# The values' weight sums, loaded and stored by GpSimd's queue instead of SyncE's

## The chip, the core and the metric

The kernel runs on one core of a Trainium2 chip. The time is the device time of one execution in microseconds (us), and the figure to compare is the median over the runs. TensorE (PE) multiplies matrices; VectorE (DVE), ScalarE (ACT) and GpSimd (POOL) work on tiles in SBUF; SyncE (SP) computes nothing and issues transfers. Each engine runs its own instructions in their written order, and they meet at semaphores.

## The reference, cut to what matters

One decoder layer on 1024 positions of width 2048. A normed input `h` is multiplied by one wide matrix `w_in`; its columns are queries, keys, values and gates of two attention branches. Only the values of branch A matter here:

```python
h = rmsnorm(x, norm_w[layer])
proj = jnp.einsum('bsd,dp->bsp', h, w_in[layer])
qa, ka, va, ga, qb, kb, vb, gb = jnp.split(proj, SPLIT_IDX, axis=-1)   # va: columns 2048 to 3071
...
oa = diff_attention(qa, ka, va, lam)        # 8 heads, causal, two softmax maps each
ob = swa_sinks_attention(qb, kb, vb, sinks) # window 128, with sinks
y = jnp.concatenate([ya, yb], axis=-1)      # both gated by silu
x = x + jnp.einsum('bsm,md->bsd', y, w_out[layer])
```

## The kernel before

All products are in float32, made of three products of high and low parts: ScalarE rounds a tile to its high part (`w_hi`), VectorE subtracts it from the raw tile (`w_lo`), TensorE multiplies high by high, low by high and high by low. A part of the weights of 128 x up to 512 numbers that is loaded and split like this is a chunk.

The product `va` (1024 x 2048 by 2048 x 1024) is done with seven half-size products in place of eight, as in Strassen's and Winograd's scheme. Both operands are cut into four quarters, and some of the seven products take sums of quarters. For the weights these sums are T1 to T4 of the code (not to be mixed up with the blocks T0 to T3 below). They are made ahead, in 8 row blocks kk = 0 to 7 of 128 rows:

- `load_v_sums(kk, h)` loads 128 rows of `w_in` (h = 0: the upper half of the matrix, h = 1: the lower one), 1024 columns, 512 KB, into half h of buffer kk % 2. The buffers are `vt_buf[0]` (the trace calls it expd) and `vt_buf[1]` (w_out_sums, a name that it shares with a later use; also tbuf in the code). From kk = 2 on a load waits until the four sums of kk - 2 are stored (`vt_stored`).
- `v_weights(kk, h)` on VectorE makes two of the four sums in place, after both loads of kk have landed (`vt_in`), and counts them in `vt_done`.
- `store_v_sums(kk, h)` waits for these and stores them to DRAM (`scr_v`, in the trace w_v_sums_dram), 512 KB in rows of 2 KB.
- `load_v(j)` later fetches each sum as the weights of a tile of the product, j = 8 m + kk.

When each of these is done is written out by a table of steps. A step s is one chunk of the projection that runs on TensorE before the first attention head (`first == -1`, steps 0 to 15, then t = 16, 17 in `v_stage`). With `V_SUM_AT = [0, 2, 4, 6, 8, 11, 12, 14]` row block kk is loaded at step `V_SUM_AT[kk]`, summed two steps later and stored three steps later. In each step SyncE issues the load of a weight chunk four steps ahead (`load_ahead`), which waits until the chunk two before it is split (`w_lo_ready`); then stores and loads of the sums; then stores of gates and of rows (`store_rows`), which wait for GpSimd or ScalarE.

In the same steps the first head's queries and keys are made, in four blocks of rows, here T0 to T3. For each, VectorE reduces squares (L2164, counts `ss_ready`) and multiplies by the norm's weights, GpSimd works out the inverse root in three small instructions (`norms`: L2453, L2455, L2457), VectorE rotates the rows (`rotate`, counts `norm_chain`), and GpSimd scales them (`scale_rows`, L2490, counts `rst_ready`), after which SyncE stores them. VectorE's reduction of the next block waits for the norm of the one before it. VectorE's own order in one step is: split of a chunk, reduction, rotation, `v_weights`, sums of the left operand. Between 84 and 304 us GpSimd has nothing else to do than these norms and scalings.

Of the kernel before, what the change touches and what calls it, by code (L numbers as in the profile page):

```python
# [39 lines left out]
P = 128  # L40
# [8 lines left out]
AW = 1024  # L49
# [84 lines left out]
def v_sum_steps(*delays):  # L134

    return {t: [(kk, h) for kk in range(HALF_K) for h in range(2) if V_SUM_AT[kk] + delays[h] == t] for t in range(48)}


V_SUM_LOADS, V_SUMS, V_SUM_STORES = v_sum_steps(0, 0), v_sum_steps(2, 2), v_sum_steps(3, 3)
# [153 lines left out]
def new_kv(k, unit):  # L293

    return k == "A" or (unit - AH) % 2 == 0
# [17 lines left out]
def decoder_layer(nc, x, positions, norm_w, w_in, q_norm_a, k_norm_a, lambda_q1, lambda_k1,  # L313
# [16 lines left out]
    scr_v = nc.dram_tensor("w_v_sums_dram", (4, 1024, 512), F32).ap()  # L330

    with ExitStack() as ctx:
# [3 lines left out]
        def sem(name):  # L336
            return ctx.enter_context(nc.semaphore(name))
# [65 lines left out]
        vt_buf = [expd[:, :, :].rearrange("p a (b c) -> p (a b) c", b=2), tbuf[:, :, :]]  # L403
# [36 lines left out]
        sm = {n: sem("s_" + n) for n in names}  # L440

        def pair(name):
            return [sem(f"s_{name}{b}") for b in range(2)]
# [12 lines left out]
        vt_in, vt_stored = pair("vt_in"), pair("vt_stored")  # L456
# [65 lines left out]
        def y_time(first, s):  # L522

            return (first - (len(KINDS) - 2)) * 16 + s
# [46 lines left out]
        def _(sp):  # L571
# [16 lines left out]
                sp.dma_start(w_raw[:, s % 2, 0:nk * P].rearrange("p (k c) -> p k c", k=nk), src)\  # L588
                  .then_inc(w_in_sem[s % 2], 16)

            def load_v_sums(kk, h):

                n, r = kk % 2, kk * P
                if kk < 2:
                    sp.wait_ge(sm["w_used"], 8)
                else:
                    sp.wait_ge(vt_stored[n], 32 * (kk // 2))
                sp.dma_start(vt_buf[n][:, 2 * h:2 * h + 2, :].rearrange("p a c -> p (a c)"),
                             w_in[0, 1024 * h + r:1024 * h + r + P, 2 * AW:3 * AW]).then_inc(vt_in[n], 16)

            def store_v_sums(kk, h):
                sp.wait_ge(sm["vt_done"], 4 * kk + 2 * h + 2)
                sp.dma_start(scr_v[2 * h:2 * h + 2, kk * P:(kk + 1) * P, :].rearrange("m r t -> r m t"),
                             vt_buf[kk % 2][:, 2 * h:2 * h + 2, :]).then_inc(vt_stored[kk % 2], 16)

            def load_v(j):

                m, kk = V_TILES[j]
                x, r = V_RIGHT[m], slice(kk * P, (kk + 1) * P)
                if j < 2:  # L610
                    sp.wait_ge(sm["norm_chain"], 6)
                    sp.wait_ge(sm["ss_ready"], 2)
                else:
                    sp.wait_ge(sm["w_lo_ready"], QV + j - 3)
                if x in V_T:
                    sp.wait_ge(vt_stored[kk % 2], 32 * (kk // 2 + 1))
                    src = scr_v[V_T[x], r, :]
                else:
                    r0, c0 = V_B[x]
                    src = w_in[0, r0 + kk * P:r0 + (kk + 1) * P, 2 * AW + c0:2 * AW + c0 + 512]  # L620
                sp.dma_start(v_raw(j), src).then_inc(wide_in[(j + 2) % 4], 16)
# [8 lines left out]
            def v_stage():  # L630
                load_v(4)
                for j in range(NV):
                    for kk, h in V_SUM_STORES.get(16 + j, ()):
                        store_v_sums(kk, h)
                    for kk, h in V_SUM_LOADS.get(16 + j, ()):
                        load_v_sums(kk, h)
                    if j + 5 < NV:
                        load_v(j + 5)
                    if j >= NV - 2:
                        load_chunk(QV + j + 2, "A", 1, j - (NV - 2))  # L640
                    if j == 48:
                        load_step("A", 0, 0)
                    for r in range(4):
                        if j == 35 + r:
                            store_v(u_y, 0, 0, r, 1 + 2 * r, "v_first_stored")
                        if j == 43 + r:
                            store_v(u_y, 0, 1, r, 9 + r, "v_first_stored")
                for q in (2, 3):
                    load_chunk(QV + NV + q, "A", 1, q)
                for r in range(4):  # L650
                    store_v(u_z, 512, 1, r, 16 + 2 * r + 1, "v_stored")
                    store_v(u_x, 512, 0, r, 16 + 2 * r + 2, "v_stored")
# [286 lines left out]
            def body(it, first):  # L939
                for s in range(16):  # L940
                    i = s // 2
                    d, ch, before = proj_tile(it, first, s)
                    t = y_time(first, s)
# [3 lines left out]
                    if first == len(KINDS) - 1 and s == 0:  # L947
                        load_step(kind(first), it, 1)
                    load_ahead(it, first, s)
                    for kk, h in V_SUM_STORES.get(s, ()) if first == -1 else ():  # L950
                        store_v_sums(kk, h)
                    for kk, h in V_SUM_LOADS.get(s, ()) if first == -1 else ():
                        load_v_sums(kk, h)
                    if first == len(KINDS) and s == 1:
                        store_y(step_at(-1, it, first), it, first)
                    if d and ch["last"] and d["kind"] != "O" and not d["turned"]:
# [1477 lines left out]
        def _(pool):  # L2434
# [34 lines left out]
                x_rms(r)  # L2469

            def v_stage():
                pool.wait_ge(sm["w_used"], QV + NV)
                for c in range(2):
                    pool.memset(kT_lo[c][half_rows[1 - c], :].bitcast(F32), 0.0).then_inc(sm["k_zeros"], 1)
                    pool.wait_ge(sm["k_zeros"], c + 1)
# [6 lines left out]
            def scale_rows(d, b):  # L2482

                if not d["norm"]:
                    return
                seq = d["K"] * 2 + b
                wait(pool, sm["norm_chain"], seq * 3 + 3)
                wait(pool, sm["rs_ready"], seq * 3 + 3)
                x3 = rows[:, b, :].rearrange("p (g c) -> p g c", g=8)
                pool.tensor_tensor(x3, x3, ss_h[:, 16:24].unsqueeze(2).to_broadcast([P, 8, HD]), ALU.mult)\  # L2490
                    .then_inc(rst_ready[b], 1)

            def lo_v(st):

                i, k = st["i"], st["k"]
                if not new_kv(k, st["unit"]):
                    return
                lo, w = (2 * P, P) if k == "A" else (3 * P, HD)
                wait(pool, sm["v_hi_ready"], v_count(k, st["unit"], i))

                dst = v_lo[:, i, :] if k == "A" else v_hi[:, i, HD:P]
                pool.tensor_tensor(dst, qkv[:, i % 2, lo:lo + w], v_hi[:, i, 0:w].bitcast(F32),
                                   ALU.subtract).then_inc(sm["v_split"], 1)

            def sum_s3(k):

# [35 lines left out]
            def body(it, first):  # L2542
                for s in range(16):
                    i = s // 2
                    cur = step_at(i, it, first)
                    back1 = step_at(i - 1, it, first)
                    last = first == len(KINDS) - 1
                    if s % 2 and last or s % 2 == 0 and cur and cur["k"] == "A" and i:
                        lo_v(cur)
                    if s % 2 and cur and cur["k"] == "B":  # L2550
                        scale_probs(cur)
                    tb = turned_before(it, first, s)
                    if tb and tb[0]["norm"]:
                        norms(tb[0], tb[2])
                    if s % 2:
                        if back1 and back1["k"] == "A":
                            wait(pool, sm["o_squared"], back1["G"] + 1)
                            inv_rms(ss_o[:, 2:3], ss_o[:, 1:2], ss_o[:, 0:1], 4, sm["o_pow"], back1["G"] * 4)
                            wait(pool, sm["o_pow"], back1["G"] * 4 + 3)
                            pool.tensor_tensor(ss_o[:, 0:1], ss_o[:, 0:1], inv_sum[:, back1["i"] % 2, 0:1], ALU.mult)\  # L2560
                                .then_inc(sm["o_pow"], 1)
                        if cur and not last and not (cur["k"] == "A" and i):
                            lo_v(cur)
                    late = norm_block_back(it, first, s, 1)
                    if tb and not norm_block_back(it, first, s, 0):
                        scale_rows(tb[0], tb[2])
                    if late:
                        scale_rows(late[0], 1)
                    for k in S3_LOWS.get(s, ()) if first == len(KINDS) - 1 else ():
                        s3_low(k)  # L2570
                    for what, k, m in sum_steps(first, s):
                        if what == "S3" and m:
                            sum_s3(k)
                        elif what == "S" and 2 <= m < 5:
                            sum_s(k, m - 2)
# [30 lines left out]
```

## Time and profile before

| | us |
|---|---|
| median of 3 runs | 1743.07 |
| lowest, highest | 1741.13, 1743.52 |
| the profiled execution | 1741.46 |
| its span | 1739.7 |
| TensorE busy | 1723.1 (99%) |
| VectorE busy | 1295.1 (74%) |
| ScalarE busy | 838.8 (48%) |
| GpSimd busy | 463.4 (27%) |

The span is the time from the first to the last recorded event of the profiled execution. A row of a timeline gives the start, the time (of a merged row the time from its start to its end), engine, line, operation, what is written and read, and the number of merged instructions; in brackets how long the engine had been idle ahead of it and what ended that. SPq is SyncE's queue of transfers: its rows are issues, not the transfer. The chain gives start, time and what: the work is followed back from the end, at each step to what released it.

### The profile page before, as it was taken

The numbers are of one execution on the slowest core, as the hardware profiler recorded it, in microseconds if no ns is written. First come the engines' busy times: TensorE is split into PE (matmuls) and PEld (weight loads), VectorE is DVE, ScalarE is ACT, GpSimd is POOL, SyncE is SP. The second block draws the span as 40 slices with busy tenths as digits, with TensorE's granted clock in tenths as the row PEclk, the third lists the DMA queues.
The fourth block names the chain that finished last, engine by engine and source line by source line (L and its number), as shares of the span: only waits on it lengthen the run. The fifth ranks groups of instructions, "written<-read, shape, count | busy, mean of one in ns | idle before, by whom it ended". The sixth has DMA issues, their size and how long they took to land.

```text
span 1739.7 us, 28224 instructions
## 1 busy us (share of the span) xinstructions
PE 1723.1 (99%) x8720; PEld 1446.2 (83%) x8720; DVE 1295.1 (74%) x2601; ACT 838.8 (48%) x2209; POOL 463.4 (27%) x661
## 2 busy tenths in 40 slices
PE   9999999999999999999999999999999999999999
PEld 8977888888888888888888888888888878888887
DVE  7788787787878787878787675876857887455754
ACT  6422432555555555656565544444445477343321
POOL 3211000332424242423333332432424325110000
PEclk9999999999999999999999999999999999999999
DMA  6288344534444444434343333452443566596654
GB/s 225 69 280 276 106 113 128 151 115 127 133 135 128 136 126 133 138 125 136 129 137 124 113 111 122 121 173 90 132 127 115 187 214 212 177 329 229 204 196 157
DMA packets 265098, 268.54 MB, mean 154 GB/s; under 512 B 26913, under 2 KB 190753, under 8 KB 263969
## 3 DMA queue, kind: packets, MB, share of 16 engines
q1 hardware_dynamic: 264992, 267.23, 48.7%
q8 instruction: 55, 0.90, 0.2%
q14 instruction: 49, 0.40, 0.1%
q10 hardware_dynamic: 2, 0.01, 0.0%
HBM read 188.52 MB, written 80.74 MB: 155 GB/s over the span
## 4 chain that ended last, share of the span: by engine, by line
PE 87%; DVE 4%; DMA 2%; ACT 1%; issue 1%; SPq 0%; POOL 0%; ACTq 0%; DVEq 0%
PE ps_a L1444 20%; PE ps_a L1446 20%; PE ps_a L1445 20%; PE ps_b L1444 4%; PE ps_b L1446 4%; PE ps_b L1445 4%; PE ps_b L1613 3%; PE ps_a L1565 3%; PE ps_b L1628 3%; PE ps_a L1564 3%; PE ps_b L1665 1%; DVE attention_parts L1856 1%; PE ps_b L1558 1%; DMA w_out_sums<-in_w_in 1%; PE ps_b L1630 1%; PE ps_b L1642 1%
## 5 line engine op out<-in xcount | busy, mean ns | idle before, releaser
L1444 PE MATMUL ps_a<-hT_hi,w_hi_sb 128*128 128x512 f32 x1280 | 522.5, 408 | 3.3 <-DVE w_lo_sb L1856 3.3
L1446 PE MATMUL ps_a<-hT_hi,w_lo_sb 128*128 128x512 f32 x1280 | 501.9, 392 | 0.0
L1445 PE MATMUL ps_a<-hT_lo,w_hi_sb 128*128 128x512 f32 x1280 | 499.0, 390 | 0.0
L1446 PEld LDWEIGHTS ps_a<-hT_hi,w_lo_sb 128*128 128x128 f32 x1280 | 240.1, 188 | 54.0
L1444 PEld LDWEIGHTS ps_a<-hT_hi,w_hi_sb 128*128 128x128 f32 x1280 | 240.9, 188 | 50.7 <-DVE w_lo_sb L1856 5.0
L1856 DVE TENSOR_TENSOR w_lo_sb<-w_raw_sb,w_hi_sb 128x512 fp32r<-128x512 f32 (+2 forms) x287 | 194.7, 680 | 115.6 <-ACT w_hi_sb L1093 60.8
L1445 PEld LDWEIGHTS ps_a<-hT_lo,w_hi_sb 128*128 128x128 f32 x1280 | 241.5, 189 | 42.6
L1300 ACT ACTIVATE attention_parts<-ps_b 128x512 fp32r<-128x512 f32 (+3 forms) x160 | 76.8, 521 | 240.2 <-PE ps_b L1613 240.2
L1856 DVE TENSOR_TENSOR ps_a<-ps_a,mask 128x128 f32<-128x128 f32 (+2 forms) x176 | 67.9, 397 | 123.2 <-PE ps_a L1565 123.2
L1093 ACT ACTIVATE w_hi_sb<-w_raw_sb 128x512 fp32r<-128x512 f32 (+1 forms) x220 | 124.2, 565 | 66.9 <-DMA w_raw_sb<-in_w_in 33.4
L1856 DVE TENSOR_TENSOR attention_parts<-ps_b,attention_parts 64x128 fp32r<-64x128 f32 (+4 forms) x304 | 130.5, 447 | 5.8 <-ACT attention_parts L1300 3.7
L2453 POOL TENSOR_TENSOR ss_o<-ss_o,small 128x1 f32<-128x1 f32 x64 | 43.3, 677 | 330.4 <-ACT ps_b L1343 330.4
L2490 POOL TENSOR_TENSOR stage_rows<-stage_rows,ss_h 128x512 f32<-128x512 f32 x50 | 65.5, 1311 | 200.7 <-DVE stage_rows L1856 200.6
L1444 PE MATMUL ps_b<-w_hi_sb,hT_hi 128*128 128x512 f32 x288 | 112.0, 389 | 0.0
L1445 PE MATMUL ps_b<-w_lo_sb,hT_hi 128*128 128x512 f32 x288 | 112.0, 389 | 0.0
L1446 PE MATMUL ps_b<-w_hi_sb,hT_lo 128*128 128x512 f32 x288 | 112.0, 389 | 0.0
L1444 PE MATMUL ps_a<-w_hi_sb,hT_hi 128*128 128x512 f32 (+1 forms) x288 | 107.1, 372 | 0.5 <-DVE hT_lo L1856 0.3
L1446 PE MATMUL ps_a<-w_hi_sb,hT_lo 128*128 128x512 f32 (+1 forms) x288 | 105.9, 368 | 0.0
L1445 PE MATMUL ps_a<-w_lo_sb,hT_hi 128*128 128x512 f32 (+1 forms) x288 | 105.8, 367 | 0.0
L2535 POOL TENSOR_TENSOR expd<-expd,inv_sum 128x1024 f32<-128x1024 f32 (+2 forms) x40 | 58.3, 1467 | 164.9 <-DVE inv_sum L2296 164.9
L1411 ACT ACTIVATE expd<-ps_a,neg_max 128x256 f32<-128x256 f32 (+7 forms) x128 | 94.9, 741 | 12.5 <-DVE neg_max L2207 7.2
L2207 DVE TENSOR_REDUCE neg_max<-ps_a 128x1 f32<-128x256 f32 (+7 forms) x128 | 97.0, 758 | 4.4
(190 smaller groups left out, 3493.9 us busy)
## 6 DMA issues: line engine op xcount, KB each, us to landing
w_raw_sb<-in_w_in SPq DMA_DIRECT2D x108, 256.0 KB, 3.0
w_out_sums<-in_w_out SPq DMA_DIRECT2D x64, 256.0 KB, 3.8
w_out_sums_dram<-w_out_sums SPq DMA_DIRECT2D x64, 256.0 KB, 2.7
w_raw_sb<-in_w_in SPq DMA_DIRECT2D x64, 192.0 KB, 2.6
qkv_sb<-qkv_a_dram SPq DMA_DIRECT2D x64, 192.0 KB, 2.6
w_out_sums<-y_dram SPq DMA_DIRECT2D x24, 512.0 KB, 5.1
qkv_a_dram<-stage_rows SPq DMA_DIRECT2D x40, 256.0 KB, 2.5
w_raw_sb<-w_out_sums_dram SPq DMA_DIRECT2D x40, 256.0 KB, 3.1
```

The source lines that it names most:

```text
L1093: act.activation(w_hi[:, b4, 0:w], w_raw[:, b4 % 2, 0:w], ACT.Copy).then_inc(sm["w_hi_ready"], 1)
L1300: act.activation(aT_hi[:, lo:hi], p_tr[bank_of(name, first)][:, 0:hi - lo], ACT.Copy).then_inc(sm["at_hi"], 1)
L1411: act.activation(expd[:, c, 0:w], flat[:, 0:w], ACT.Exp, bias=neg_max[:, c:c + 1], accum_out=sums[:, c:c + 1]).then_inc(sm["x_done"], 1)
L1444: pe.matmul(dst, a_hi, b_hi, start=start, stop=False)
L1445: pe.matmul(dst, a_hi, b_lo, start=False, stop=False)
L1446: return pe.matmul(dst, a_lo, b_hi, start=False, stop=stop)
L1564: pe.matmul(dst, q, k, start=start, stop=False)
L1565: return pe.matmul(dst, q, k_lo, start=False, stop=stop)
L1856: return dve.tensor_tensor(o, a, b, op)
L2207: dve.tensor_reduce(neg_max[:, c:c + 1], flat[:, 0:(i + 1) * P], AX, ALU.max, negate=True)\
L2490: pool.tensor_tensor(x3, x3, ss_h[:, 16:24].unsqueeze(2).to_broadcast([P, 8, HD]), ALU.mult)\
L2535: pool.tensor_tensor(part, part, scale.to_broadcast([P, heads.stop - heads.start, 256 - lo]), ALU.mult).then_inc(sm["probs_scaled"], 1)
```

## The change

The functions `load_v_sums` and `store_v_sums` are moved word for word from SyncE's program to GpSimd's, with `sp` replaced by `pool`, and so are the places where they are called. In a step they stood behind `load_ahead` on SyncE; on GpSimd they stand at the end of the step's norms and scalings, and the last two steps' stores at the start of its `v_stage`. The waits and semaphores are the same, and so are all other instructions.

```diff
 # SyncE's program
-            def load_v_sums(kk, h):
-            ...
-            def store_v_sums(kk, h):
-            ...
             def v_stage():
                 load_v(4)
                 for j in range(NV):
-                    for kk, h in V_SUM_STORES.get(16 + j, ()):
-                        store_v_sums(kk, h)
-                    for kk, h in V_SUM_LOADS.get(16 + j, ()):
-                        load_v_sums(kk, h)
...
                     load_ahead(it, first, s)
-                    for kk, h in V_SUM_STORES.get(s, ()) if first == -1 else ():
-                        store_v_sums(kk, h)
-                    for kk, h in V_SUM_LOADS.get(s, ()) if first == -1 else ():
-                        load_v_sums(kk, h)
...
 # GpSimd's program
             def v_stage():
+                for t in range(16, 18):
+                    for kk, h in V_SUM_STORES.get(t, ()):
+                        store_v_sums(kk, h)
...
+            def load_v_sums(kk, h):
+
+                n, r = kk % 2, kk * P
+                if kk < 2:
+                    pool.wait_ge(sm["w_used"], 8)
+                else:
+                    pool.wait_ge(vt_stored[n], 32 * (kk // 2))
+                pool.dma_start(vt_buf[n][:, 2 * h:2 * h + 2, :].rearrange("p a c -> p (a c)"),
+                             w_in[0, 1024 * h + r:1024 * h + r + P, 2 * AW:3 * AW]).then_inc(vt_in[n], 16)
+
+            def store_v_sums(kk, h):
+                pool.wait_ge(sm["vt_done"], 4 * kk + 2 * h + 2)
+                pool.dma_start(scr_v[2 * h:2 * h + 2, kk * P:(kk + 1) * P, :].rearrange("m r t -> r m t"),
+                             vt_buf[kk % 2][:, 2 * h:2 * h + 2, :]).then_inc(vt_stored[kk % 2], 16)
...
                     if late:
                         scale_rows(late[0], 1)
+                    if first == -1:
+                        for kk, h in V_SUM_STORES.get(s, ()):
+                            store_v_sums(kk, h)
+                        for kk, h in V_SUM_LOADS.get(s, ()):
+                            load_v_sums(kk, h)
```

GpSimd after the change, steps 7 to 9: T1's norm (three instructions), stores of kk = 2, T1's scaling, loads of kk = 4, stores of kk = 3:

```order
L2430 TENSOR_TENSOR ss_h<-ss_h,small 128x8 [waits s_ss_ready]
L2432 TENSOR_TENSOR ss_h<-ss_h,small 128x8 [waits s_rs_ready]
L2434 TENSOR_TENSOR ss_h<-ss_h,small 128x8 [waits s_rs_ready]
L2497 DMA w_v_sums_dram<-expd 128x2x512 [waits s_vt_done] x2
L2470 TENSOR_TENSOR stage_rows<-stage_rows,ss_h 128x512 [waits s_rs_ready,s_norm_chain]
L2492 DMA expd<-in_w_in 128x1024 [waits s_vt_stored0] x2
L2497 DMA w_v_sums_dram<-w_out_sums 128x2x512 [waits s_vt_done] x2
```

Before, only the norm's three instructions and the scaling stood here, with nothing between them. Now the stores of kk = 2 come behind T1's norm, and the loads of kk = 4 behind T1's scaling.

GpSimd after the change, steps 12 to 16: loads of kk = 6, T3's norm and scaling, stores of kk = 5, loads of kk = 7, stores of kk = 6 and 7:

```order
L2492 DMA expd<-in_w_in 128x1024 [waits s_vt_stored0] x2
L2430 TENSOR_TENSOR ss_h<-ss_h,small 128x8 [waits s_ss_ready]
L2432 TENSOR_TENSOR ss_h<-ss_h,small 128x8 [waits s_rs_ready]
L2434 TENSOR_TENSOR ss_h<-ss_h,small 128x8 [waits s_rs_ready]
L2470 TENSOR_TENSOR stage_rows<-stage_rows,ss_h 128x512 [waits s_rs_ready,s_norm_chain]
L2497 DMA w_v_sums_dram<-w_out_sums 128x2x512 [waits s_vt_done] x2
L2492 DMA w_out_sums<-in_w_in 128x1024 [waits s_vt_stored1] x2
L2497 DMA w_v_sums_dram<-expd 128x2x512 [waits s_vt_done] x2
L2497 DMA w_v_sums_dram<-w_out_sums 128x2x512 [waits s_vt_done] x2
```

The stores of kk = 5 now stand behind T3's scaling, which waits for VectorE's rotation (`norm_chain`).

SyncE before the change, steps 11 to 14 (L598 loads and L603 stores of the sums, L588 chunks, L621 the first summed weights, L830 rows):

```order
L588 DMA w_raw_sb<-in_w_in 128x4x128 [waits s_w_lo_ready] x2
L603 DMA w_v_sums_dram<-expd 128x2x512 [waits s_vt_done] x2
L598 DMA w_out_sums<-in_w_in 128x1024 [waits s_vt_stored1] x2
L621 DMA gate_y<-w_v_sums_dram 128x512 [waits s_vt_stored0,s_ss_ready,s_norm_chain]
L598 DMA expd<-in_w_in 128x1024 [waits s_vt_stored0] x2
L830 DMA qkv_a_dram<-stage_rows 128x4x128 [waits s_rst_ready0]
L621 DMA gate_y<-w_v_sums_dram 128x512 [waits s_vt_stored1,s_ss_ready,s_norm_chain]
L621 DMA w_raw_sb<-w_v_sums_dram 128x512 [waits s_vt_stored0,s_w_lo_ready]
L603 DMA w_v_sums_dram<-w_out_sums 128x2x512 [waits s_vt_done] x2
L598 DMA w_out_sums<-in_w_in 128x1024 [waits s_vt_stored1] x2
```

After the change the rows of L598 and L603 are gone from it, and the others follow each other directly. The stores of kk = 4 (the first L603) stood behind two chunks there, and those of kk = 5 (the second) behind summed weights only.

## Rows read from the trace of the kernel before

**Rows 1.** The page: busy us and share of the span, by engine.
```profile
PE 1723.1 (99%) x8720; PEld 1446.2 (83%) x8720; DVE 1295.1 (74%) x2601; ACT 838.8 (48%) x2209; POOL 463.4 (27%) x661
```
**Rows 2.** Timeline of PE: the matmuls with idle time ahead of them, 90 to 160 us.
```profile
94.10 0.50 PE L1444 MATMUL ps_a<-hT_hi,w_hi_sb 128*128 128x512 f32 x1 [0.48 <-DVE w_lo_sb L1856]
...
118.85 0.50 PE L1444 MATMUL ps_a<-hT_hi,w_hi_sb 128*128 128x512 f32 x1 [0.36 <-DVE w_lo_sb L1856]
...
128.54 0.50 PE L1444 MATMUL ps_a<-hT_hi,w_hi_sb 128*128 128x512 f32 x1 [0.71 <-DVE w_lo_sb L1856]
...
149.54 0.80 PE L1444 MATMUL ps_a<-w_hi_sb,attention_parts 128*128 128x512 f32 x1 [2.54 <-DVE w_lo_sb L1856]
...
158.59 0.50 PE L1444 MATMUL ps_a<-w_hi_sb,attention_parts 128*128 128x512 f32 x1 [0.58 <-DVE w_lo_sb L1856]
```
**Rows 3.** Busy time by stretch: length, PE, PEld, DVE, ACT, POOL, clock, DMA share, GB/s.
```profile
145.00:150.00 5.00, 2.46 (x10) 1.78 (x9) 4.90 (x8) 1.64 (x3) 1.28 (x1) 0.90 0.39 113
150.00:155.00 5.00, 5.00 (x18) 3.95 (x18) 3.21 (x6) 0.63 (x1) 0.00 (x0) 0.76 0.99 354
...
175.00:200.00 25.00, 25.00 (x112) 20.71 (x111) 20.38 (x32) 10.69 (x19) 0.00 (x0) 1.00 0.38 107
```
**Rows 4.** The chain of work, 110 to 160 us: start, us, what.
```profile
111.46 5.19 DMA w_v_sums_dram<-expd
117.05 5.89 DMA expd<-in_w_in
...
128.93 0.51 SPq L603
...
131.05 7.43 DMA w_out_sums<-in_w_in
...
141.41 5.76 DMA w_v_sums_dram<-w_out_sums
147.57 5.41 DMA w_out_sums<-in_w_in
153.00 0.70 DVE w_out_sums L1856
...
157.93 0.60 DVE w_lo_sb L1856
```
**Rows 5.** Timeline of SyncE's queue: stores and loads of the sums, and one chunk.
```profile
94.50 1.00 SPq L603 DMA_DIRECT2D w_v_sums_dram<-expd  x2
...
99.42 0.82 SPq L598 DMA_DIRECT2D expd<-in_w_in  x2
...
110.94 0.98 SPq L603 DMA_DIRECT2D w_v_sums_dram<-expd  x2
...
128.51 0.37 SPq L588 DMA_DIRECT2D w_raw_sb<-in_w_in  x1
...
139.96 1.82 SPq L603 DMA_DIRECT2D w_v_sums_dram<-w_out_sums  x2
```
**Rows 6.** Timeline of POOL: a scaling at 83 us, T1's power, T2's and T3's scaling.
```profile
82.78 1.46 POOL L2490 TENSOR_TENSOR stage_rows<-stage_rows,ss_h 128x512 f32<-128x512 f32 x1
...
111.74 2.05 POOL L2457 TENSOR_TENSOR ss_h<-ss_h,small 128x8 f32<-128x8 f32 x1
...
134.74 1.43 POOL L2490 TENSOR_TENSOR stage_rows<-stage_rows,ss_h 128x512 f32<-128x512 f32 x1 [0.45 <-DVE stage_rows L1856]
...
144.85 1.43 POOL L2490 TENSOR_TENSOR stage_rows<-stage_rows,ss_h 128x512 f32<-128x512 f32 x1 [6.46 <-DVE stage_rows L1856]
```
**Rows 7.** Timeline of DVE: sums of kk = 3, 4 and 5, T3's last rotation.
```profile
114.87 3.59 DVE L1856 TENSOR_TENSOR w_out_sums<-w_out_sums 128x512 f32<-128x512 f32 x4
...
122.96 2.87 DVE L1856 TENSOR_TENSOR expd<-expd 128x512 f32<-128x512 f32 x4 [3.56 <-DMA expd<-in_w_in]
...
138.51 2.87 DVE L1856 TENSOR_TENSOR w_out_sums<-w_out_sums 128x512 f32<-128x512 f32 x4 [1.79 <-DMA w_out_sums<-in_w_in]
...
144.02 0.75 DVE L1856 TENSOR_TENSOR stage_rows<-stage_rows,ps_b 128x256 f32<-128x256 f32 x2
```

More of the change, by code:

```diff
@@ L589, in load_chunk @@
                   .then_inc(w_in_sem[s % 2], 16)
-            def load_v_sums(kk, h):
[L593 to L599, printed above, removed]
-            def store_v_sums(kk, h):
-                sp.wait_ge(sm["vt_done"], 4 * kk + 2 * h + 2)
-                sp.dma_start(scr_v[2 * h:2 * h + 2, kk * P:(kk + 1) * P, :].rearrange("m r t -> r m t"),
-                             vt_buf[kk % 2][:, 2 * h:2 * h + 2, :]).then_inc(vt_stored[kk % 2], 16)
             def load_v(j):
```

## The prediction

> **What bounds the kernel now.** I read the busy table first, then TensorE's idle stretches, then the chain of work through the stage that the change touches, and last the queues of SyncE, VectorE and GpSimd there. TensorE is busy for 1723.1 of 1739.7 us [rows 1], so the kernel can only gain or lose where TensorE waits. The changed transfers all lie between 85 and 157 us. There TensorE has five waits of note, all for VectorE's low parts of weights: 0.48, 0.36, 0.71, 2.54 and 0.58 us [rows 2], 4.67 us together. From 175 us on it is busy for 25.00 of 25 us again [rows 3], so whatever delay stands at about 160 us is carried to the end whole, and a gain could be 4.67 us at the very most (and little more for the clock).
>
> What stands behind these waits is the chain [rows 4]. It does not run through TensorE there, but through the sums themselves: the stores of kk = 2 land after 5.19 us, the loads of kk = 4 that waited for them land after 5.89, VectorE sums kk = 4, the stores of kk = 4 go out at 128.93, the loads of kk = 5 land 7.43 us after 131.05, the sums of kk = 5 start at 138.51 [rows 7], their stores land 5.76 us after 141.41, the loads of kk = 7 land 5.41 us after 147.57, the sums of kk = 7 start at 153.00, and the low part for which TensorE waits follows at 157.93. VectorE runs in its written order, so a late load holds all splits of weights behind it. The path is thus a ping-pong of two buffers (load, sum, store, load), and a step of it that is issued later is paid by TensorE almost one for one.
>
> **What is moved.** 16 loads and 16 stores of 512 KB go from SyncE's queue to GpSimd's. Instructions, bytes and waits are the same; nothing is added. What changes is (a) what each issue costs the engine, and (b) what stands ahead of it in the queue.
>
> (a) The price of an issue. A pair costs SyncE 0.98 to 1.00 us, so 0.5 each [rows 5]. The rows have no DMA issued by GpSimd. From below the nearest row is SyncE's 0.5; from above GpSimd's own instructions: 1.43 for 128x512, 2.05 for a tiny power [rows 6]. I take 1.0, about midway between SyncE's 0.5 and the 1.43, and keep 0.5 and 2.05 for the range. A transfer can hardly be under way before its descriptors are made, so I let it also land 0.5 us later than SyncE's did, counted from its issue. The Trainium skill (DMA: Bandwidth & Descriptors, Specifications) puts the first byte at about 1 us for a DMA issued by GpSimd and 0.6 for one by SyncE; no row here shows it, and with it each landing would be 0.4 later instead of 0.5, and the sum below 0.4 less, over four landings.
>
> (b) The queue, step by step. T1 to T3 are the second to fourth blocks of rows whose norms GpSimd works out; it does a norm (three small instructions) and later a scaling of the rows, each after a wait for VectorE.
>
> Step 1, kk = 0 and 1: GpSimd is free at 84.2 [rows 6], about when they are due, and the loads of both row blocks go out at once, where SyncE had two chunks between them. TensorE had waited 0.48 for the low part behind the sums of kk = 0 [rows 2]. Value: between -0.48 and +0.5 (more transfers in flight beside the weight chunks); I take 0.
>
> Step 2, stores of kk = 2: before at 110.94 [rows 5]. Now they stand behind T1's norm, whose last instruction ends at 111.74 + 2.05 = 113.8 [rows 6]. Second store issued at 114.8; landed 5.19 + 0.5 later, 120.5. Loads of kk = 4: second at 121.5, landed 5.89 + 0.5 later, 127.9. Before, the sums started at 122.96, as the load landed [rows 4, 7]: **+4.9**. VectorE had waited 3.56 us for exactly this load, so nothing hides it; TensorE's wait of 0.71 at 128.54 grows by it.
>
> Step 3, kk = 4 to 5: the sums take 2.9 [rows 7], the second store goes at 130.8, the loads of kk = 5 at 131.8 and 132.8. Here the move gives something back: a weight chunk issued only at 128.51 stood ahead on SyncE [rows 5], though the sums of kk = 4 were done at 122.96 + 2.87 = 125.8. The loads land at 139.2 (with 5.89) to 140.7 (with 7.43). VectorE was ready for kk = 5 at 138.51 - 1.79 = 136.7 [rows 7], now 136.7 + 4.9 = 141.6. So kk = 5 starts at 141.6 instead of 138.51, **+3.1**: 1.8 us of the lateness are swallowed by the idle time that was there.
>
> Step 4, the largest: stores of kk = 5. SyncE issued them at 139.96 and 141.4, as soon as their halves were summed [rows 4, 5]. On GpSimd they stand behind the scaling of T3, which waits for VectorE's rotation of T3, and VectorE does that only after the sums of kk = 5: the rotation ended at 144.77 [rows 7] and the scaling ran from 144.85 for 1.43 us [rows 6]. Shifted by 3.1, the scaling ends at 149.4. Stores at 149.4 and 150.4 instead of 141.4: even with no shift from steps 2 and 3 the second would be at 147.3, 5.9 us late.
>
> Step 5, kk = 7: with the landing of [rows 4] (5.76 + 0.5) the loads go at 156.7 and 157.7 and land, with 5.41 + 0.5, at 163.6 instead of 153.00, +10.6. But those landings were measured in a crowd (DMA share 0.99 in 150 to 155, [rows 3]); the spread-out schedule has fewer transfers at once, and stores issued at 94.50 had landed by 99.42, 4.4 us after the second [rows 5]. With 4.4 in place of 5.76 it is +9.2. I take **+9.2** for the start of the sums of kk = 7, and for the low part behind it and the matmul that waited 0.58 for it.
>
> The loads of kk = 6 now stand behind T2's scaling, which ran at 134.74 [rows 6] and moves to 139.6, so they go at about 141; but VectorE comes to kk = 6 only after T3's rotation, at about 148, when they have landed: nothing. T2's rows on SyncE wait some 4 us longer for their scaling, and three loads of summed weights behind them; TensorE's second product needs the next of these at 149.5 and later: nothing, or at most a part of the 3.1 that is counted.
>
> The clock: after the wait of 2.54 us TensorE's granted clock was 0.90 and then 0.76 on the mean [rows 3], so for a while at its lower level of 1.2 GHz; it cost (1 - 0.76) x 5 = 1.2 us, hidden since TensorE then waited for VectorE anyway. After a wait of some 7 us at 160 the same stretch is likely, and VectorE is then the limit for two or three steps: 0 to 1.2, I take 0.3.
>
> Sum: 0 + 9.2 + 0.3 = **+9.5 us**. The profiled execution took 1741.46 us (span 1739.7 and 1.8 around it), the median is 1743.07; on the median that is 1752.6, and I say 1752.5.
>
> With an issue of 0.5 and no later landing the same steps give +2.9 at kk = 4, +1.1 at kk = 5 and +6.6 at kk = 7 (+5.2 with the quick landing); with 2.05 and 1.55 later landings they give +9.1, +8.1 and +19.6.
>
> **Rivals.**
>
> *Dear issue.* GpSimd's port or program makes an issue cost 2 us or more. For it: VectorE's four sums take 3.59 us beside a GpSimd instruction and 2.87 without [rows 7], so the two do hinder each other, and VectorE is nearly always busy here. Against it: 0.7 us per case is small. Price +14 to +20, 1757 to 1763. The Trainium skill (SBUF — State Buffer, SBUF: two separate sides) has a rule that speaks against this change: while VectorE runs an operation in a two-port mode, GpSimd can't write descriptors and its DMAs starve. Such operations don't stand in this stretch as far as the rows tell (0.70 us for 512 columns in the chain), so by the page's own condition it should not bite. By the rule the time would be the same 1757 to 1763.
>
> *Only the issuer changes.* The landing times don't move enough to matter, because GpSimd issues at once where SyncE had stood, and the crowd thins: within 3.5 us. It needs step 4 to be wrong by half, which only much faster transfers (3 us from issue to landing) would bring; no row has that. The Trainium skill (DMA: Bandwidth & Descriptors, Issuing engines are not separate DMA queues) says that spreading DMAs over issuing engines saves nothing but issue time, which would be this rival; the rows say that it is the place in the queue that counts. Time 1742 to 1746.
>
> *Faster.* The chunk at 128.51 held kk = 5's loads by up to 4 us; with them earlier, the waits of 2.54 and 0.58 go, -3.1, 1740. This decides if kk = 4's loads leave no later than 117.05; but T1's norm stands ahead of the stores that free their buffer. I see no way round it, save that VectorE reaches T1 several us earlier. That the edit does nothing is no case: the written order of GpSimd has the 32 transfers, and SyncE's has lost them.
>
> **Chances.** Forecast (+4.5 to +14) 0.71; dear issue 0.12; no change 0.10; faster 0.07. A measurement of this kernel can tell 0.2%, 3.5 us, from no change. Faster 0.07, within 0.2% 0.10, slower 0.83. The range leaves out the faster case, part of the middle one and the end of the dear one: 1746 to 1760.
>
> **What would show it.** In the changed trace: GpSimd's issues of about 1 us; stores of kk = 2 at 113.8, after T1's power; VectorE's wait before the sums of kk = 4 grown from 3.56 to some 8 us; stores of kk = 5 right behind T3's scaling, near 149; the sums of kk = 7 near 162, with VectorE idle for about 9 us ahead of it, and TensorE idle for some 7 us at 165. From 175 us on, both traces should run in parallel. I am wrong if GpSimd's transfers land much faster or slower than SyncE's, or if its issue holds VectorE up.

## The result, and the profile after

| | before | after |
|---|---|---|
| median, us | 1743.3 | 1760.94 |
| lowest, highest | 1741.13, 1744.15 | 1759.67, 1764.17 |
| ratio to before, 95% interval | | 1.0109, 1.0097 to 1.0121 |
| profiled execution, its span | 1741.46, 1739.7 | 1759.67, 1757.9 |

The change costs 17.6 us, where +9.5 was forecast and 1746 to 1760 us was the range. The direction was right, the size wrong by a factor of 1.9. The page of the changed kernel, its busy times and queues:

```profile
PE 1727.2 (98%) x8720; PEld 1449.4 (82%) x8720; DVE 1295.1 (74%) x2601; ACT 838.6 (48%) x2209; POOL 484.0 (28%) x693
...
q1 hardware_dynamic: 258336, 250.45, 45.4%
q0 software_dynamic: 4608, 16.78, 2.7%
```

VectorE does the same work in the same 1295.1 us. TensorE is busy for 4.1 us more [rows 1], though it runs the same matmuls: that is time at the lower clock. A second queue has appeared, q0, with the 16.78 MB that left q1. TensorE's idle stretches of the changed kernel, the same view as [rows 2]:

```profile
93.36 0.79 PE L1421 MATMUL ps_a<-hT_hi,w_hi_sb 128*128 128x512 f32 x1 [2.59 <-DVE w_lo_sb L1833]
...
137.28 0.80 PE L1421 MATMUL ps_a<-hT_hi,w_hi_sb 128*128 128x512 f32 x1 [5.30 <-DVE w_lo_sb L1833]
...
158.06 0.50 PE L1421 MATMUL ps_a<-w_hi_sb,attention_parts 128*128 128x512 f32 x1 [0.65 <-DVE w_lo_sb L1833]
...
174.76 0.79 PE L1421 MATMUL ps_a<-w_hi_sb,attention_parts 128*128 128x512 f32 x1 [9.60 <-DVE w_lo_sb L1833]
```

Together 18.1 us, against 4.7 before: 13.5 more idle and 4.1 more busy make 17.6 of the 18.2 us by which the span grew. The last of them is the matmul that waited 0.58 at 158.59 before; it starts 16.2 us later. The first was not forecast at all: 2.59 us at 93, where 0.48 stood. The chain through the stage, as [rows 4]:

```profile
84.34 7.83 DMA w_raw_sb<-in_w_in
...
92.19 0.53 ACT w_hi_sb L1070
...
115.20 2.09 POOL ss_h L2434
...
117.34 0.70 issue
118.04 5.94 DMA w_v_sums_dram<-expd
...
124.86 6.82 DMA expd<-in_w_in
131.71 0.70 DVE expd L1833
...
153.38 1.43 POOL stage_rows L2470
154.81 0.75 POOL w_v_sums_dram L2497
...
155.56 3.96 DMA w_v_sums_dram<-w_out_sums
159.52 0.29 issue
159.81 0.56 POOL w_out_sums L2492
160.38 8.79 DMA w_out_sums<-in_w_in
...
169.19 0.70 DVE w_out_sums L1833
...
174.11 0.61 DVE w_lo_sb L1833
```

Both places that the prediction named are there: T1's power at 115.20 directly ahead of the stores of kk = 2, and T3's scaling at 153.38 directly ahead of those of kk = 5. Two pieces are longer than the forecast had them: a weight chunk, issued at 84.34, that takes 7.83 us to land (a transfer that the change does not touch; before, it was split 3.2 us after its issue), and loads of kk = 7 that take 8.79, where 5.9 was taken.

What an issue costs GpSimd, in its timeline:

```profile
83.79 1.32 POOL L2492 DMA_DIRECT2D expd<-in_w_in  x2
85.10 1.05 POOL L2492 DMA_DIRECT2D w_out_sums<-in_w_in  x2
...
117.25 1.52 POOL L2497 DMA_DIRECT2D w_v_sums_dram<-expd  x2
```

A row with x2 holds two issues. The median is 0.55 us for a load and 0.73 for a store, less than the 1.0 that was taken. So the rival of the dear issue is not what happened, although the time fell on its price.

### The profile page after: what moved, and what is told of

Its sections match the earlier page's. It is cut to its first block, busy times and chain, and to the rows that moved or that the text cites. A ratio compares the mean times of both kernels' runs of the same rounds, so it can differ in the third digit from the quotient of the medians.

```text
span 1757.9 us, 28224 instructions
## 1 busy us (share of the span) xinstructions
PE 1727.2 (98%) x8720; PEld 1449.4 (82%) x8720; DVE 1295.1 (74%) x2601; ACT 838.6 (48%) x2209; POOL 484.0 (28%) x693
## 3 DMA queue, kind: packets, MB, share of 16 engines
q0 software_dynamic: 4608, 16.78, 2.7%
## 4 chain that ended last, share of the span: by engine, by line
PE 86%; DVE 4%; DMA 3%; issue 1%; ACT 1%; POOL 1%; SPq 0%; ACTq 0%; DVEq 0%; POOLq 0%
PE ps_a L1421 20%; PE ps_a L1423 20%; PE ps_a L1422 19%; PE ps_b L1423 4%; PE ps_b L1421 4%; PE ps_b L1422 4%; PE ps_b L1590 3%; PE ps_a L1542 3%; PE ps_b L1605 3%; PE ps_a L1541 3%; PE ps_b L1642 1%; PE ps_b L1535 1%; PE ps_b L1607 1%; DMA qkv_sb<-qkv_a_dram 1%; DVE attention_parts L1833 1%
```

## The experiments

The theories. P, place: the stores stand behind a norm or a scaling on GpSimd and leave late (the prediction's own). R, ring: GpSimd's transfers travel on a queue of their own, beside SyncE's and not in line with it, and push aside SyncE's weight chunks, for which TensorE then waits. Each ratio is to the kernel before, with its 95% interval. The kernel before was run again beside each group of experiments (medians 1742.61, 1743.39 and 1742.45 us), and a difference in us is to the median of the same group unless the text says otherwise.

### Only the first four loads moved

k01_pool is the kernel before with four loads on GpSimd. Their landings are counted on a pair of semaphores of their own, which the lines below do not show.

```diff
 # k01_pool: SyncE's loads of the sums only from step 3 on
-                    for kk, h in V_SUM_LOADS.get(s, ()) if first == -1 else ():
+                    for kk, h in V_SUM_LOADS.get(s, ()) if first == -1 and s > 2 else ():
 # GpSimd, behind the scalings of the step
+                    if first == -1 and s <= 2:
+                        for kk, h in V_SUM_LOADS.get(s, ()):
+                            load_v_sums(kk, h)
```

> The kernel before with one part of the change: only the four loads of kk = 0 and 1 go out on GpSimd, behind the second scaling at 84 us; all other transfers of the sums stay on SyncE. Theory R (a ring of its own): GpSimd's transfers share the 16 DMA engines with SyncE's ring in turns of packets, and rows of 4 KB push aside a weight chunk with rows of 512 B. Then the chunk issued at 84.7 lands after 7 to 8 us instead of 3, TensorE waits 2 to 3 us near 93 instead of 0.48, and the whole is 3 to 4 us longer: ratio 1.002. Theory P (only the place behind norms and scalings matters): nothing is behind a norm here, the chunk lands in 3 us, 0 to -1 us.

Measured: 1746.21 us, ratio 1.0022 (1.0012 to 1.0031), so +3.6 us in the medians. The chain of this kernel:

```profile
84.59 7.81 DMA w_raw_sb<-in_w_in
92.40 0.02 issue
92.42 0.53 ACT w_hi_sb L1093
92.95 0.02 issue
92.97 0.57 DVE w_lo_sb L1856
```

The chunk was issued at 84.59, and its landing took 7.81 us. In the kernel before it was issued at 84.74 and split by ScalarE at 87.92, 3.2 us later, and the chunk behind it at 91.36:

```profile
84.74 0.44 SPq L588 DMA_DIRECT2D w_raw_sb<-in_w_in  x1
...
87.92 0.53 ACT L1093 ACTIVATE w_hi_sb<-w_raw_sb 128x384 fp32r<-128x384 f32 x1 [8.44 <-DMA w_raw_sb<-in_w_in]
91.36 0.53 ACT L1093 ACTIVATE w_hi_sb<-w_raw_sb 128x384 fp32r<-128x384 f32 x1 [2.92 <-DMA w_raw_sb<-in_w_in]
```

Theory R holds: 4 of 32 transfers, none behind a norm, cost a fifth of the whole. All the other kept traces with these loads on GpSimd show the same landing: 7.83 us in the changed kernel, 8.07 in after_stores_first, 8.18 in loads_pool. A rival is the order in time, since GpSimd's first load was issued at 84.03, ahead of the chunk. It is too small: at the 377 to 407 GB/s that the engines moved between 88 and 92 us, 512 KB take some 1.3 us (an estimate from these figures), and the chunk came 4.6 us later.

```diff
 # k01_act: the same four by ScalarE, ahead of its split of the first chunk below
+                    if first == -1 and s == 1:
+                        act.wait_ge(rst_ready[1], 1)
+                        for kk, h in ((0, 0), (0, 1), (1, 0), (1, 1)):
+                            load_v_sums(kk, h)
```

> As the run before, but the four loads of kk = 0 and 1 are issued by ScalarE at 84 us (it waits for the same scaling). Theory R in its general form (any second ring): the chunk lands after 7 to 8 us and TensorE waits 2 to 3 us near 93, as with GpSimd; 3 to 4 us longer. If only GpSimd's transfers push others aside (R for descriptors made by software): the chunk lands in 3 to 4 us, within 1 us of before.

Measured: 1742.6 us, ratio 0.9999 (0.999 to 1.0009). The timeline of ScalarE (ACTq are its issues):

```profile
84.09 0.94 ACTq L1104 DMA_DIRECT2D expd<-in_w_in  x2
85.07 1.63 ACTq L1104 DMA_DIRECT2D w_out_sums<-in_w_in  x2
89.45 0.53 ACT L1093 ACTIVATE w_hi_sb<-w_raw_sb 128x384 fp32r<-128x384 f32 x1 [10.33 <-DMA w_raw_sb<-in_w_in]
94.30 0.52 ACT L1093 ACTIVATE w_hi_sb<-w_raw_sb 128x384 fp32r<-128x384 f32 x1 [4.33 <-DMA w_raw_sb<-in_w_in]
```

Between the two expectations: the chunk of 84.56 landed by 89.4, in 4.9 us, later than before but 3 us sooner than beside GpSimd's loads, and the next one, issued at 85.05, only at 94.3 (in k01_pool 94.4, issued at 85.08). The matmul behind that second chunk started at 95.47, 1.4 us later than before (94.10), but the time of the whole is that of before within 0.1%. The short wait there, 0.37 us, is in part luck of this execution: TensorE's granted clock was 0.50 between 84 and 86 us (1.00 in the profiled execution of before), which brought it to the chunks about 1.6 us late. k01_pool and the changed kernel show the same 0.50 there, so their waits near 93 show the chunk less late than it was. A second queue does slow SyncE's chunks; GpSimd's held the first one for longer than ScalarE's did.

```diff
 # k01_sync: the same four by SyncE, all in step 0
-                    for kk, h in V_SUM_LOADS.get(s, ()) if first == -1 else ():
+                    for kk, h in ((0, 0), (0, 1), (1, 0), (1, 1)) if first == -1 and s == 0 else ():
                         load_v_sums(kk, h)
 # and V_SUM_LOADS as before from step 4 on
```

> As before, all on SyncE, but the loads of kk = 1 are issued right behind those of kk = 0 in step 0, so the same 2 MB are asked for at about 85 us, behind one chunk and ahead of the next two in one ring. Theory R: the chunk issued at 84.7 stands ahead and lands in 3 us; the next two stand behind 2 MB and land near 93; TensorE's wait near 94 is 1 to 2 us; +0.5 to +1.5 us in all. Theory Q (the amount in flight, whatever the ring): the first chunk lands after 7 to 8 us as well, +3 to +4 us.

Measured: 1744.41 us, ratio 1.0013 (1.0003 to 1.0023). SyncE's issue of the first chunk and ScalarE's split of it:

```profile
83.89 0.44 SPq L588 DMA_DIRECT2D w_raw_sb<-in_w_in  x1
...
86.82 0.53 ACT L1097 ACTIVATE w_hi_sb<-w_raw_sb 128x384 fp32r<-128x384 f32 x1 [8.42 <-DMA w_raw_sb<-in_w_in]
```

In one queue the order of issue holds: the first chunk, ahead of the loads, was split 2.9 us after its issue; the next, behind them, landed 7.88 us after 86.41, and TensorE waited 2.70 us at 95.5, more than the 1 to 2 expected. The time lost (1.8 us, by the interval 0.5 to 4.0) is a little above what R gave and half of what Q did; the time alone does not separate them, the landing of the first chunk decides against Q. With the same 2 MB asked for, the second chunk was split at 94.3 or 94.4 in all three runs. What differs is how early the first one, issued at 83.89, 84.56 or 84.59, gets through: 86.8 from one queue with the loads behind it, 89.4 beside ScalarE's loads, 92.4 beside GpSimd's.

### The place on GpSimd

```diff
 # after_stores_first: the changed kernel, the stores of a step first
+                    for kk, h in V_SUM_STORES.get(s, ()) if first == -1 else ():
+                        store_v_sums(kk, h)
                     tb = turned_before(it, first, s)
                     if tb and tb[0]["norm"]:
                         norms(tb[0], tb[2])
 ...
                     if first == -1:
-                        for kk, h in V_SUM_STORES.get(s, ()):
-                            store_v_sums(kk, h)
                         for kk, h in V_SUM_LOADS.get(s, ()):
```

> The changed kernel with the stores of the sums moved ahead of the norm and the scalings of their step on GpSimd; the loads stay where the change put them. Theory P: the stores of kk = 2 go when their sums are done (113.6 instead of 117.3) and those of kk = 5 too (near 149 instead of 154.8), which takes 3.6 us off the start of kk = 4 and 5 off that of kk = 7: 5 to 8 us shorter than the changed kernel, 1753 to 1756 us, ratio to before 1.006 to 1.007. Theory R alone: the stores' place is worth 0 to 2 us, 1759 to 1761, ratio 1.009 to 1.010.

Measured: 1751.43 us, ratio 1.005 (1.0034 to 1.0067): 9.5 us shorter than the median of the changed kernel, 8.8 if each is taken against the kernel before of its own group. The stores of kk = 5 now go ahead of T3's scaling:

```profile
148.32 0.78 POOL L2497 DMA_DIRECT2D w_v_sums_dram<-w_out_sums  x1
149.31 0.73 POOL L2497 DMA_DIRECT2D w_v_sums_dram<-w_out_sums  x1 [0.20 <-issue]
152.49 1.41 POOL L2470 TENSOR_TENSOR stage_rows<-stage_rows,ss_h 128x512 f32<-128x512 f32 x1 [2.45 <-DVE stage_rows L1833]
```

at 149.31 instead of 155.56, and the sums of kk = 7 start at 161.62 instead of 169.19. Place is worth about half of the 17.6, a little more than P expected, but not where P had it. At kk = 4 it gave back 1.0 us and not 3.6 (sums at 130.68 instead of 131.71): the second store of kk = 2 left at 115.46 instead of 118.04 and took 8.65 us to land instead of 5.94. At kk = 7 it gave more, since the loads land in 5.48 us in place of 8.79 (DMA share 0.84 while they ran, 0.96 in the changed kernel).

```diff
 # stores_pool: the changed kernel's stores on GpSimd, the loads back on SyncE
 # stores_pool_first: the same, the stores ahead of the norms as above
 # loads_pool: the changed kernel's loads on GpSimd, the stores back on SyncE
```

> Half of the change: the stores of the sums on GpSimd in the places of the change (behind norms and scalings), the loads on SyncE as before. Theory P (place): the stores of kk = 2 are behind T1's norm and those of kk = 5 behind T3's scaling, as in the changed kernel; +3 at kk = 4, +5 at kk = 7 or a little more, so 7 to 10 us longer than before (ratio 1.004 to 1.006). Theory R (GpSimd's loads push SyncE's chunks aside): no load is on GpSimd, so no chunk is late: 0 to 2 us.

Measured: 1754.23 us, ratio 1.006 (1.0044 to 1.0077), +10.8. That is a little over P's upper end. TensorE waits 3.67 at 132.8 and 7.80 at 169.4, for kk = 4 and kk = 7, and nothing at 93.

> As the run before, but the stores stand ahead of their step's norm and scalings on GpSimd. Theory P: they go when their sums are done, as fast as before or sooner (kk = 1 and 4 had stood behind a chunk on SyncE): -3 to +1 us, ratio 0.998 to 1.001. If a store issued by GpSimd lands later or pushes chunks aside by itself: +2 to +5 us.

Measured: 1739.74 us, ratio 0.9983 (0.9973 to 0.9992), **3.7 us faster than the kernel before**. The stores go as their sums are done (125.70 for kk = 4, where SyncE had them at 128.93), and with no load on its queue a store from GpSimd lands like SyncE's: 4.90, 5.19 and 4.16 us in the chain.

> The other half: the loads of the sums on GpSimd in the places of the change, the stores on SyncE as before. Theory R: the chunk at 84.6 lands after 8 us (TensorE waits 2.6 us), and the chunk behind the loads of kk = 5 is late again by some 4 us: 6 to 9 us longer (ratio 1.0035 to 1.005). Theory P alone: the loads' places cost little (kk = 3 and 6 stand behind a scaling, at most 1 us shows): 0 to 2 us.

Measured: 1755.44 us, ratio 1.0068 (1.0051 to 1.0084), +12.1: more than R's 6 to 9. The chain has the chunk (8.18 us) and slow loads, but also stores that SyncE issues late because its chunks are late:

```profile
83.94 8.18 DMA w_raw_sb<-in_w_in
...
116.08 7.34 DMA w_v_sums_dram<-expd
...
123.70 0.64 POOL expd L2498
...
124.34 7.61 DMA expd<-in_w_in
...
154.75 1.42 POOL stage_rows L2476
...
156.20 0.64 POOL w_out_sums L2498
...
156.84 7.32 DMA w_out_sums<-in_w_in
```

The loads of kk = 7 stand behind T3's scaling here (154.75). P's sum had given that no price, as the stores were thought to be the last to come. Each half of the change costs 11 to 12 us, the whole 17.6, so the halves must hide in part behind each other.

### Undoing in the changed kernel

```diff
 # after_k01_sync: the changed kernel, the loads of kk = 0 and 1 on SyncE again
 # after_both: the same, and the stores ahead of the norms
```

> The changed kernel, with the loads of kk = 0 and 1 back on SyncE in their old places. Theory R: the chunk at 84.6 lands in 3 us again, TensorE's wait near 93 is 0.5 instead of 2.6, and the 3.6 us that this part alone cost come off: 1757 us, ratio 1.0085. If the first delay is swallowed by the later ones: 1760 to 1761, ratio 1.010.

Measured: 1758.66 us, ratio 1.009 (1.0073 to 1.0107), -2.3 in the medians; the chunk of 84.06 lands in 3.14 us again. The two intervals overlap, so this alone does not tell -3.6 from -1. The profiled executions, each the shortest of its four (1755.89 and 1759.67 us), show the whole of it: the matmul behind kk = 4 starts at 133.55 instead of 137.28 (its wait is longer, 6.23 for 5.30, since TensorE comes to it sooner), the one behind kk = 7 at 170.77 instead of 174.76. The other three took 1758.6 to 1759.3 us, so it stays open whether the whole comes back every time.

> The changed kernel with two parts undone at once: the stores ahead of the norms and scalings, and the loads of kk = 0 and 1 back on SyncE. If the two causes add up, the 9.5 us that the first gave and the 2.3 that the second gave come off the 17.6: +5.8 us, ratio 1.003 to 1.004. What is left is then theory R at the chunk behind the loads of kk = 4 and 5 (its landing 6 to 7 us instead of 3.1). If place was all that was left, 0 to 1 us.

Measured: 1749.88 us, ratio 1.0042 (1.0027 to 1.0058): +7.4, where adding up gave +5.8. R is a part of what is left. In the timeline of GpSimd, 109 to 112 us:

```profile
109.01 1.17 POOL L2504 DMA_DIRECT2D w_out_sums<-in_w_in  x2
110.16 0.74 POOL L2509 DMA_DIRECT2D w_v_sums_dram<-expd  x1
111.36 0.74 POOL L2509 DMA_DIRECT2D w_v_sums_dram<-expd  x1 [0.45 <-DVE expd L1845]
```

Loads and stores of 2 MB go out within 3 us on GpSimd's queue. In the timelines of ScalarE and then of TensorE:

```profile
120.88 1.16 ACT L1082 ACTIVATE w_hi_sb<-w_raw_sb 128x256 fp32r<-128x256 f32 x2 [10.55 <-DMA w_raw_sb<-in_w_in]
```

```profile
121.81 0.79 PE L1433 MATMUL ps_a<-hT_hi,w_hi_sb 128*128 128x512 f32 x1 [2.83 <-DVE w_lo_sb L1845]
```

The chunk issued at 111.43 is split at 120.88, and the second store lands 9.25 us after 111.36. The only difference from stores_pool_first is that the loads of kk = 2 to 7 are GpSimd's: -3.7 there, +7.4 here, each against the kernel before of its own group, so these twelve loads cost about 11 us. How much of it is the queue and how much their place behind norms and scalings is not shown; no run has them on GpSimd ahead of these.

### A version that beats both

```diff
 # sync_stores_early: everything on SyncE
-                    load_ahead(it, first, s)
                     for kk, h in V_SUM_STORES.get(s, ()) if first == -1 else ():
                         store_v_sums(kk, h)
+                    load_ahead(it, first, s)
                     for kk, h in V_SUM_LOADS.get(s, ()) if first == -1 else ():
 # sync_early5: as above, and in step 11 the loads ahead of load_ahead too
```

> The kernel before with all transfers on SyncE, and the stores of the sums ahead of the step's weight chunk instead of behind it. If the gain of the stores on GpSimd ahead of the norms (ratio 0.9983) comes from the stores going when their sums are done, SyncE gives it too: kk = 4's stores at 124 to 126 instead of 128.9, 1 to 4 us less, ratio 0.998 to 0.9995. If it comes from the second queue (SyncE never held up by a store's wait), it does not: the chunks then wait behind the stores, ratio 0.9995 to 1.001.

Measured: 1739.18 us, ratio 0.9981 (0.9972 to 0.999), 3.3 us faster than the kernel before. SyncE gives the whole gain that the stores on GpSimd gave; it was the order, not the engine. TensorE's waits of 2.54 and 0.58 have become 0.67 at 147.4 and none at 155, and its clock is 1.00 in both stretches of [rows 3]:

```profile
145.00:150.00 5.00, 4.33 (x19) 3.27 (x18) 4.93 (x9) 1.64 (x3) 0.00 (x0) 1.00 1.02 393
150.00:155.00 5.00, 4.86 (x22) 3.71 (x21) 4.86 (x8) 0.76 (x2) 0.00 (x0) 1.00 1.00 356
```

> As the run before, and the loads of kk = 5 also ahead of the chunk of step 11: they go at about 127 instead of 130. If the way kk = 4, 5, 7 is what TensorE waits for at 149.5 and 158.6, this takes 2 to 4 us off the kernel before (ratio 0.998 to 0.999). If the pushed-back chunk takes its place, no gain over the run before.

Measured: 1739.19 us, ratio 0.9981 (0.9972 to 0.999): no gain over the run before. VectorE reaches the sums of kk = 5 at 135.43 after other work and does not wait for their load; nor did it in the run before (136.36, with no idle time ahead of it), so bringing the load forward buys nothing.

## Why the prediction was off

**(a) The price of an issue**, 1.0: too dear, it is 0.55 and 0.73. By this step alone the time would have been forecast too long, not too short.

**Step 1 failed.** It put the first loads at 0 and bounded them by +0.5. They cost 3.6 us (k01_pool). The text saw "more transfers in flight beside the weight chunks" and gave it no mechanism: as long as all came from SyncE, a chunk issued first landed first. On GpSimd's queue 2 MB are served beside it. In the changed kernel T1's power stands at 115.20 instead of 111.74, and all that follows carries these 3.5 us: the late chunk and, after the wait for it, a stretch at the lower clock (0.50 between 94 and 96 us, 1.00 before). The Trainium skill (DMA: Bandwidth & Descriptors, Queues, rings and completion order) says that each DMA engine goes round its queues packet by packet; by that the chunk shares the engines with what another queue holds, and the trace agrees: 7.81 us beside GpSimd's loads, 2.9 ahead of the same loads in one queue. The prediction had cited another section of that page of the Trainium skill, that the issuing engine only changes the issue time; k01_pool, with the same bytes and +3.6 us, shows that it is not all.

**Step 2 was right**: +4.9 forecast; measured 131.71 - 122.96 = 8.75, of which 3.5 come from step 1 and 5.3 from the step. The norm ahead of the stores is where it was put, and the landings (5.94 and 6.82) are near the 5.7 and 6.4 that were taken. It was right for the changed kernel only: without the norm ahead of them (after_stores_first) the stores landed so much later that only 1.0 us came back.

**Step 3 failed.** 1.8 us were to be given back before kk = 5 (+3.1). The sums of kk = 5 start 147.05 - 138.51 = 8.5 us late, against 8.75 at kk = 4: 0.2 given back. VectorE's idle time there was eaten by waits that are not in the rows of before: 0.92 and 0.77 us for ScalarE at 144 to 146, since the chunk issued behind the loads of kk = 5 was split only at 143.65, and since TensorE, at its lower clock after the wait of 5.30, came late to T3's transposes:

```profile
144.32 0.76 DVE L1833 TENSOR_TENSOR w_lo_sb<-w_raw_sb,w_hi_sb 128x512 fp32r<-128x512 f32 x1 [0.92 <-ACT w_hi_sb L1070]
145.84 0.69 DVE L2141 TENSOR_REDUCE ss_h<-ps_b 128x8 f32<-128x512 f32 x1 [0.77 <-ACT ps_b L1213]
```

**Step 4 was right.** The second store of kk = 5 goes at 155.56 instead of 141.41, 14.2 late; less the 8.5 already there, 5.6, and 5.9 was forecast. after_stores_first takes it back: there this store goes 3.2 us after the sums of kk = 5 begin, in the changed kernel 8.5, before 2.9.

**Step 5 was mis-sized.** The stores landed even faster than the quick landing that was taken (3.96 against 4.9), but the loads of kk = 7 took 8.79 us, not 5.9. The argument was that a spread-out schedule has fewer transfers at once. It was wrong here, and the likely reason, read from the traces and not tried by itself, is that other transfers came due while kk = 7 waited. In 158 to 162 us SyncE issued gates, T3's rows and two summed weights, and GpSimd the stores of kk = 6; the DMA share was 0.94 and 0.98 in the two stretches from 160 to 170. In after_stores_first, where the loads go 4.3 us earlier, they land in 5.48.

**The clock** was put at +0.3, and this was too little as well. TensorE was busy 4.1 us longer in all. In the stretches around the two long waits the granted clock was on the mean 0.50 (135 to 140), 0.50 (170 to 175) and 0.65 (175 to 180); part of that was hidden by waits, and after the last wait 8 matmuls start 0.43 us apart instead of 0.23, 1.6 us that nothing hides.

The lateness at the start of the sums of kk = 7 adds up like this; the matmul behind them is as late:

| term | measured, us | forecast, us |
|---|---|---|
| step 1, first loads | 3.5 | 0 |
| step 2, stores of kk = 2 | 5.3 | 4.9 |
| step 3, kk = 4 to 5 | -0.2 | -1.8 |
| step 4, stores of kk = 5 | 5.6 | 5.9 |
| landing of these stores, 3.96 for 5.76 | -1.8 | -0.9 |
| from their landing to the second load | 0.5 | 0.6 |
| landing of the loads of kk = 7, 8.79 for 5.41 | 3.4 | 0.5 |
| together (rounded terms) | 16.2 | 9.2 |
| clock | 1.6 | 0.3 |

That is 17.8 of the 18.2 us by which the span grew; the rest is not explained. Of the 8.3 us by which the forecast fell short, 3.5 are step 1, 2.9 the loads of kk = 7, 1.6 step 3 and 1.3 the clock; the other terms together take about 1 off.

The rivals: the dear issue gave the right time for a reason that is not there, and VectorE did not starve GpSimd's descriptors: its stores' issues take 0.71 to 0.81 us whether VectorE runs (0.74 at 94.93) or waits (1.47 for two at 160.91), as the condition of the rule on SBUF's port, which the prediction takes from the Trainium skill (SBUF — State Buffer, SBUF: two separate sides), had let expect. "Only the issuer changes" and "faster" did not happen. The faster case held one thing that is so: the chunk at 128.51 did cost 3 us, and sync_stores_early collects them where a norm does not stand in the way.

## What to carry to other kernels

A transfer moved to another engine's queue changes two orders: it waits behind that engine's computing, and it leaves the line in which it had stood, so that it now competes with transfers that were served before it. Look for both: what stands ahead of it in the new program, and which small transfer on the old queue is awaited soon after it. If a queue holds a transfer up, moving it ahead of the waiting instruction may give the same gain with no second queue.

## What the hardware showed that was not expected

A chunk of 192 KB in rows of 512 B took 7.81 us to land beside 2 MB of GpSimd's loads in rows of 4 KB, 4.9 beside the same loads from ScalarE, and 2.9 when it stood ahead of them in SyncE's queue. Why GpSimd's loads weigh more than ScalarE's is open. The number of packets is not the reason: the four loads make 576 packets on GpSimd's queue (k01_pool) and 576 on ScalarE's (k01_act), as many as left SyncE's. Only the stores change: the 16 of them make 2304 packets from GpSimd and 4352 from SyncE (stores_pool). An issue costs GpSimd 0.55 us for 128 rows of 4 KB and 0.73 for 256 rows of 2 KB (medians), less than its own power of 8 numbers a row (2.05).
